# Expert blocks of a two-layer mixture-of-experts trunk: gathers issued ahead of scatters, first ring loads unheld, down weights in longer runs

## The reference

```
xf = rmsnorm(h)                                   # rows x 1024
group  = argmax(xf @ w_rg + b_rg)                 # one of 4
expert = top-2 of (xf @ w_re + b_re) in the group # 2 of its 8
for each of the 32 experts e, for the rows that chose it:
    y = (silu(xb @ w_gate[e]) * (xb @ w_up[e])) @ w_down[e]
h = h + sum over both choices of gate * y
```

## Time and profile before

| what | value |
|---|---|
| time, median of 3 runs (lowest to highest) | 1787.91 us (1786.61 to 1793.66) |
| profiled execution, span from first to last instruction | 1788.1 us |
| TensorE matmul busy | 1394.1 us (78%) |
| VectorE, ScalarE, GpSimd busy | 22%, 19%, 12% |
| DMA | 472.55 MB, mean 264 GB/s |
| blocks of layer 0, first to last matmul (lines 909 to 930) | 273.5 to 808 us |
| blocks of layer 1 | 1231.2 to 1757.1 us |

### The profile page before, as it was taken

One profiled execution on the slowest core, in us unless ns is written; L12 is line 12 of the kernel. 1 busy time (PEld: TensorE's weight loads), 2 busy tenths in 40 slices (PEclk: granted clock), 3 DMA queues, 4 the chain that ended last, 5 costly groups with the idle time before them and its releaser, 6 DMA issues. The chain is left out here.

```text
span 1788.1 us, 17867 instructions
## 1 busy us (share of the span) xinstructions
PE 1394.1 (78%) x6689; PEld 777.8 (43%) x6689; DVE 389.0 (22%) x721; ACT 344.4 (19%) x662; POOL 217.9 (12%) x380
## 2 busy tenths in 40 slices
PE   5999967877778778774999878886787777777872
PEld 5998843222222222223667756673222222222320
DVE  3335240000000000004422477432000000000003
ACT  5123210000000000005534355320000000000002
POOL 2000001111111111111000131101111111111111
PEclk9999978889889898896999899987988988989886
DMA  9022247999999999975121200335999999999983
GB/s 346 8 95 75 102 154 298 415 389 376 385 383 385 389 374 392 389 285 194 47 84 58 95 1 1 153 115 212 416 395 389 380 387 383 379 386 374 388 343 148
DMA packets 101299, 472.55 MB, mean 264 GB/s; under 512 B 10528, under 2 KB 10604, under 8 KB 68480
## 3 DMA queue, kind: packets, MB, share of 16 engines
q1 hardware_dynamic: 86864, 441.48, 63.9%
q0 software_dynamic: 14384, 30.36, 4.6%
HBM read 465.17 MB, written 23.13 MB: 273 GB/s over the span
## 5 line engine op out<-in xcount | busy, mean ns | idle before, releaser
L909 PE MATMUL ps<-ring,act 128*64 128x512 f32 x1984 | 437.0, 592 | 0.0
L930 PE MATMUL ps<-ring,act 128*64 128x512 f32 x992 | 311.4, 784 | 34.3 <-ACT act L723 34.3
L876 PE MATMUL ps<-parts 128*128 128x512 f32 (+1 forms) x1104 | 270.2, 404 | 7.2 <-DVE parts L1164 6.6
L909 PEld LDWEIGHTS ps<-ring,act 128*64 128x64 f32 x1984 | 154.9, 137 | 270.8 <-issue 270.8
L876 PEld LDWEIGHTS ps<-parts 128*128 128x128 f32 (+1 forms) x1104 | 197.1, 181 | 70.0 <-issue 6.8
L916 PE MATMUL ps<-const,nat 128*128 128x128 f32 x256 | 47.7, 311 | 217.5 <-DMA nat<-hn_rows,src_now 217.5
L1347 DVE TENSOR_TENSOR act<-act,ps 128x256 f32<-128x256 f32 x64 | 27.0, 422 | 790.2 <-ACT act L721 790.2
L930 PEld LDWEIGHTS ps<-ring,act 128*64 128x64 f32 x992 | 96.1, 184 | 210.6 <-issue 210.6
L916 PEld LDWEIGHTS ps<-const,nat 128*128 128x128 f32 x256 | 36.3, 209 | 270.4 <-issue 270.4
L862 PE MATMUL ps<-parts 128*128 128x264 f32 x1152 | 144.3, 287 | 4.5 <-DVE parts L1159 2.9
L862 PEld LDWEIGHTS ps<-parts 128*128 128x128 f32 x1152 | 143.0, 191 | 5.5 <-issue 5.5
(11 more groups left out here) (162 smaller groups left out, 868.3 us busy)
## 6 DMA issues: line engine op xcount, KB each, us to landing
ring<-in_e_gate SPq DMA_DIRECT2D x62, 2048.0 KB, 9.2
ring<-in_e_up SPq DMA_DIRECT2D x62, 2048.0 KB, 13.7
ring<-in_e_down SPq DMA_DIRECT2D x62, 2048.0 KB, 10.9
ring<-in_a_w_in SPq DMA_DIRECT2D x6, 2048.0 KB, 19.9
ring<-in_w_kv SPq DMA_DIRECT2D x4, 2048.0 KB, 10.6
arena<-expert_rows POOLq DMA_DIRECT2D x16, 512.0 KB, 7.4
ring<-in_a_w_out SPq DMA_DIRECT2D x2, 2048.0 KB, 8.0
arena<-in_e_up SPq DMA_DIRECT2D x2, 2048.0 KB, 13.2
```

Of the source, the lines that this page charges most:

```text
L876: last = mm(bank, x[:, k, :], w[:, k, :], start=(k == 0 and i == 0), stop=(k == KC - 1 and i == 2))
L909: last = mm(ps[f * C:(f + 1) * C, 2 + b, :].rearrange("p (g n) -> p g n", g=2), x, w, start=(k == 0), stop=(k == KC - 1))
L930: last = mm(ps[o * C:(o + 1) * C, 6 + b, :], hT[:, b, (2 * c + a) * C:(2 * c + a + 1) * C], w[:, f * D + o * DH:f * D + (o + 1) * DH], sta ...
```

## The change

Four edits. (1) On GpSimd the gather of block e+2 is issued before the scatter of block e, and waits for the turn of block e rather than of block e+1. (2) SP no longer waits for the stored rows or the first gathers before the first ring loads of a layer. (3) The down weights are read as `(a p c) n`: partition p takes two neighbouring rows in each half of the matrix, two runs of 8 KB. (4) To match, the transposes of the hidden rows take every second column rather than 128 neighbouring ones.

```diff
                 if part == "down":
-                    sp.dma_start(dst.rearrange("p (k n) -> p k n", k=FC), w.rearrange("(f p) n -> p f n", p=P)).then_inc(landing, 16)
+                    sp.dma_start(dst.rearrange("p (a m) -> p a m", a=2), w.rearrange("(a p c) n -> p a (c n)", a=2, c=FC // 2)).then_inc(landing, 16)
...
-                nt = tiles_of(layer)
-                sp.wait_ge(hn_stored[layer][(nt - 1) % 2], 16 * ((nt + 1) // 2))
                 load((0, 0), "down", None)
-                for b in range(2):
-                    sp.wait_ge(gathered[layer][b], 16)
                 for part in ORDER:
                     load((0, 1), part, None)
...
                     for u in range(2):
                         n = q * 4 + 2 + 2 * u if not last else q * 4 + 2 + u
+                        if not last:
+                            pool.wait_ge(x_turned, E * layer + q * 2 + u + 1)
+                            gather(u, q * 2 + u + 2, n)
+                            n = n + 1
                         pool.wait_ge(y_ready, E * layer + q * 2 + u + 1)
...
-                        if not last:
-                            pool.wait_ge(x_turned, E * layer + q * 2 + u + 1)
-                            gather(u, q * 2 + u + 2, n + 1)
...
-                    last = nc.tensor.transpose(ps[:, 4 + b, c * P:(c + 1) * P], hidden[:, b, c * P:(c + 1) * P], ident)
+                    last = nc.tensor.transpose(ps[:, 4 + b, c * P:(c + 1) * P], hidden[:, b, c:FE // 2:2], ident)
```

## The result

| | median | runs | profiled span |
|---|---|---|---|
| before | 1788.64 us | 1786.61 to 1793.66 (4) | 1788.1 us |
| changed | 1711.17 us | 1710.12 to 1712.09 (4) | 1708.5 us |

The ratio is 0.9567, 95% interval 0.9546 to 0.9589: 77 us faster (74 to 81). Run twice more beside before, the changed kernel gained 84.5 and 79.4 us (1705.79 and 1707.86 us). I had forecast 1689, 99 us faster, with a range of 1670 to 1740. The changed kernel's profiled execution took 1710.32 us, 1.8 us more than its span, so some 2 us of the distance between 1689 and 1711 is only that I compared a span with a time.

A forecast was written before the change was run, and what follows sets the result against it. The gather's dependence loop was taken as the bound at 17.1 us a block, with DMA next at 15.5. Savings of 48.6 us in layer 0 and 50.4 in layer 1, together 99.0, took 1788.1 to 1689 us; range 1670 to 1740.

The forecast's parts named there:

- The circle through the gather: Expert loop: down load, scatter, gather, TensorE products wait in turn; 6.1 + 11.0 = 17.1 us a block, 8.6 after the change.
- DMA's full share was not a limit: Expert loops: share 0.99 at 382 GB/s meant slow packets and short gaps; a deep queue needs 15.7 us a block.
- W, the DMA time of an expert: DMA time to load one expert with a deep queue, the new bound: 15.5 us, bounds 15.0 and 15.7.
- the longer runs: Down weight loads in runs of 8 KB instead of 4 KB: 0.2 us less DMA time a block.
- TensorE's own block: TensorE's own work on a block of the expert loop: 11.9 us at full clock, up to 13.6.
- First gather: First gather of each layer, slowed by loads beside it: 3.1 us late in layer 0, 1.0 in layer 1.
- the unheld loads: First weight loads of a layer, issued without waiting for stored rows or first gathers: gain 0.
- Every second column: Strided weight load of the hidden-row transposes: 0.12 us a block, 7.6 us over 64 blocks, covered by TensorE's weight wait: 0.
- The slow clock at the last product: End of each layer's expert loop: TensorE starts the last gate/up product at slow clock after idling, costing 1.7 us.
- Rival C: Gathers queue behind the deep load ring, up to 26.9 us each: 19.0 us a block, 1894 us in all; chance 0.03.
- the other rule: Skill rule that HBM binds HBM-to-SBUF loads at about 358 GB/s a core: 18.2 us a block, nothing to gain.

## Why the prediction was right, and where it was off

**The circle through the gather.** Right. The wait is gone, and edit 1 alone gives 76 us, nearly the whole. Its sum of 6.1 and 11.0 was right for the kernel before, but as a law it was too stiff: half an up load less moved both terms.

**DMA's full share was not a limit.** Right, and the main thing. The share was 0.99 before and 1.01 after, at 382 and 420 GB/s.

**W, the DMA time of an expert.** This is the term that was mis-sized: 15.5 forecast, 15.8 measured. Two parts. I read the 15.7 for 4 KB runs from one distance in the first blocks. In every kernel with the new order the distances repeat expert by expert, in layer 0 light ones first: edit 1 alone has 15.8, 15.6, 15.9 and 15.7 in blocks 5 to 8 of layer 0, later up to 16.45, mean 15.96. Why they differ was not tried one by one; the number of routed rows is the likely cause, since with gathers that bring nothing the distances of blocks 6 to 30 of layer 0 lie between 15.15 and 15.68 us, with full ones between 15.47 and 16.30. And the longer runs gave 0.15 us, not 0.2. Together 0.26 + 0.05 = 0.31, over 56 blocks 17 us, of the 22 us that the two layers in the table fall short. Most of the remaining 5 us is the same term, counted as the prediction has it, from landing to landing. The up loads of experts 3 and 31 of layer 1, changed kernel:

```profile
1206.67 0.41 SPq L414 DMA_DIRECT2D ring<-in_e_up  x1
...
1639.13 0.46 SPq L414 DMA_DIRECT2D ring<-in_e_up  x1
```
```profile
ring<-in_e_up SPq DMA_DIRECT2D x1, 2048.0 KB, 12.4
...
ring<-in_e_up SPq DMA_DIRECT2D x1, 2048.0 KB, 23.8
```

They landed at 1219.1 and 1662.9: 28 W = 443.8, so W = 15.85. That is 9.8 us more than the 434.0 forecast, and layer 1 falls 9.6 short. In layer 0 the same 9.8 leaves 2.6 of 12.4, of which 1.1 us is that the gate load of expert 3 was issued 31.5 us after the first gather, not 27.3 + 3.1; the rest is open.

**TensorE's own block** was forecast at 11.9 us at full clock and is 12.5 (12.57 with edit 4). I had left out that without the gather's wait TensorE waits for VectorE's hidden rows, 23.6 us in all in the waits view, 0.37 a block. It changed nothing, as the loads take longer.

**First gather.** Forecast 3.1 and 1.0 us late; it was 3.5 us in layer 0 (issue to turn 6.66 against 3.18) and 0.1 in layer 1 (1.3 in the changed kernel's last profile). That nothing would be gained by the unheld loads was right; their 3 us are in the traces; on the old order the median shows a loss too.

**Every second column.** Covered, as forecast, and 0.07 us a block rather than 0.12: TensorE has a wait for weights in most blocks (44 times in the waits view, and 6 more before a gate/up product that it puts down to "issue"). On the old order, with no cover, edits 3 and 4 together were a loss that I had not seen: I had called a cost of the longer runs excluded because gate and up have them, and looked only at the load itself, not at the gather beside it.

**The slow clock at the last product.** Forecast 1.7 us a layer, measured 1.6: 8.70 and 8.61 us for a product that takes 7.09 at full clock. That both came is partly luck: in each of the changed kernel's two later profiles one of these two products took 7.09.

**The stage ahead of layer 0**, -2.7 us, was not in the forecast and is not the change's. From 176 to 202 us (the first output projection, after TensorE idled 3.2 us) the kernel before and the changed one have

```profile
176.00:202.00 26.00, 24.91 (x97) 20.11 (x98) 9.32 (x9) 7.97 (x10) 0.55 (x1) 0.87 0.43 176
```
```profile
176.00:202.00 26.00, 25.67 (x115) 21.04 (x116) 11.08 (x12) 8.83 (x13) 0.55 (x1) 1.00 0.40 166
```

a granted clock of 0.87 and 1.00. The changed kernel's later profiles have 0.93 and 0.87 there, and their first gathers at 266.1 and 268.2 us, so this goes with the run.

**Rival C.** Out: a gather takes 6.8 us with three or more loads ahead of it in the other queue. Of the two sentences of the Trainium skill's "DMA: Bandwidth & Descriptors", section "Queues, rings and completion order", the turn-taking between queues is the one that this fits. The 425 GB/s of the Trainium skill's "HBM Reference" page, which stand in its section "Specifications (TRN2)" and not in the one that I named, are near the 420 measured; the 358 of the other rule is not the limit here.

## What to carry to other kernels

A DMA share near 1 does not say that DMA is the bound: compare the GB/s with a stretch where the queue is deep, and look at how long before its use a load lands. A small transfer inside a circle of dependences costs its whole latency each turn; issue it one turn earlier before tuning anything else, because edits that help a full queue (3 and 4, 11 us gained) can hurt the circle (14 us lost). A cost per block read from the first blocks of a loop with unequal work needs the mean over the loop.

## What the runs showed of the hardware

- With a thin load queue and scatter and gather beside it, the 16 DMA engines delivered 382 GB/s at a share of 0.99, and 416 with the same loads and a deep queue. What in the thin queue slows the packets stays open.
- Down runs of 8 KB in place of 4 KB: 420 against 416 GB/s with a deep queue; a gather beside them 6.6 against 6.1 us to landing in the old order (medians of six; 6.33 against 6.19 in the mean of 54), 6.7 to 6.8 either way in the new.
- TensorE after an idle of 3.24 us took 8.78 us for the 32 matmuls of a gate/up product (granted clock 0.80 in that stretch), after 1.05 us 7.09 (1.00). But after another idle of 3.24 us, at 595.64, it took 7.09. In the changed kernel's profile 31 products follow an idle of over 2.6 us: 23 took 8.6 to 10.1 us, 8 took 7.1. After shorter idles all took 7.1, but for the first of a layer.
- A gather of some 33 rows of 4 KB took 3.0 us to landing alone, 6.8 beside a load queue with three or more loads ahead, and cost 0.46 us a block of that queue's time.
